# Gated delta block: one unscaled split of the residual for all projections, the norm's root multiplied in behind each projection

## The reference, cut to what matters

```python
def rmsnorm_2(x, g):
    y = xf * lax.rsqrt(jnp.mean(xf * xf, axis=-1, keepdims=True) + NORM_EPS)
    return y * g

hn = rmsnorm_2(h, pre_norm[0])
proj = hn @ w_in                      # q, k, v, z and the rows b, a
qkv = silu(causal_conv(qkv, conv_w))  # 4 taps, per channel
q, k = l2norm(q) * GDN_DK ** -0.5, l2norm(k)
beta, g = sigmoid(b), -exp(a_log) * softplus(a + dt_bias)
o = gated_delta_rule_chunked(q, k, v, beta, g)
return (rmsnorm(o) * silu(z)) @ w_out
```

## Time and profile before

| | |
|---|---|
| median of 3 runs | 1937.38 us (1934.7 to 1939.07) |
| the profiled execution | 1939.72 us, of which the span of the page is 1937.6 us |
| busy: PE, DVE, ACT, POOL | 95%, 52%, 43%, 35% of the span |
| the chain that ended last | PE 45%, DVE 6%, POOL 4%, issue 3%, ACT 3% |
| MLP ends, entry begins | 739.4 us |
| groups 0 to 3 begin on DVE | 770.25, 930.71, 1087.83, 1249.25 us |

### The profile page before, as it was taken

The page is one execution under the profiler, slowest core; times in us unless marked ns, Lnnn a source line. Parts: engine busy times, 40 slices in busy tenths (PEclk is TensorE's granted clock), DMA queues, the critical chain, the costliest instruction groups (busy, mean ns, idle before and its releaser), DMA issues.

```text
span 1937.6 us, 30475 instructions
## 1 busy us (share of the span) xinstructions
PE 1832.4 (95%) x11573; PEld 1530.8 (79%) x11709; DVE 1000.4 (52%) x1762; ACT 828.4 (43%) x1512; POOL 675.3 (35%) x429
## 2 busy tenths in 40 slices
PE   6999999999999998998999999999988999999996
PEld 4777788878787876896989998998876667777776
DVE  6522233641211125665765774775766556566666
ACT  4565652352323233633633642562545433333433
POOL 3222244353534342270280263255224222222312
PEclk9999999999999998999999999999999989999998
DMA  5111223232323230420230131132122111211211
GB/s 186 55 55 57 63 93 107 73 93 71 120 76 108 76 109 22 129 87 1 79 83 30 55 91 48 52 82 76 45 100 76 55 33 55 66 56 52 76 32 44
DMA packets 73669, 138.91 MB, mean 72 GB/s; under 512 B 30640, under 2 KB 42416, under 8 KB 73296
## 3 DMA queue, kind: packets, MB, share of 16 engines
q1 hardware_dynamic: 72976, 132.41, 22.6%
q10 hardware_dynamic: 576, 4.87, 0.6%
HBM read 127.62 MB, written 9.63 MB: 71 GB/s over the span
## 4 chain that ended last, share of the span: by engine, by line
PE 45%; DVE 6%; POOL 4%; issue 3%; ACT 3%; DMA 0%; SPq 0%; ACTq 0%; POOLq 0%; DVEq 0%
PE ps L349 9%; PE ps L351 8%; PE ps L350 8%; PE ps L3131 4%; PE ps L3087 2%; PE ps L3094 2%; POOL wsp L344 2%; PE ps L3121 1%; PE ps L2804 1%; POOL ov L855 1%; PE ps L2913 1%; PE ps L2946 1%; PE ps L2951 1%; DVE aux_f L1814 1%; PE ps L2938 1%
## 5 line engine op out<-in xcount | busy, mean ns | idle before, releaser
L344 POOL TENSOR_TENSOR wsp<-raw,wsp 128x1024 fp32r<-128x1024 f32 x228 | 549.5, 2416 | 1152.9 <-ACT wsp L339 1152.6
L349 PE MATMUL ps<-h_split,wsp 128*128 128x264 f32 (+2 forms) x1552 | 536.3, 346 | 15.8 <-DVE h_split L498 5.2
L350 PE MATMUL ps<-h_split,wsp 128*128 128x264 f32 (+2 forms) x1552 | 517.0, 333 | 0.0
L351 PE MATMUL ps<-h_split,wsp 128*128 128x264 f32 (+2 forms) x1552 | 516.3, 333 | 0.0
L349 PEld LDWEIGHTS ps<-h_split,wsp 128*128 128x128 f32 x1552 | 295.0, 190 | 57.3 <-issue 16.2
L350 PEld LDWEIGHTS ps<-h_split,wsp 128*128 128x128 f32 x1552 | 295.7, 191 | 29.2 <-issue 0.5
L351 PEld LDWEIGHTS ps<-h_split,wsp 128*128 128x128 f32 x1552 | 294.8, 190 | 29.3
L339 ACT ACTIVATE wsp<-raw 128x1024 fp32r<-128x1024 f32 x228 | 237.6, 1050 | 95.3 <-PE ps L351 94.5
L349 PE MATMUL ps<-y_split,wsp 128*128 128x512 f32 (+2 forms) x512 | 196.4, 383 | 11.5 <-DVE y_split L532 5.3
L350 PE MATMUL ps<-y_split,wsp 128*128 128x512 f32 (+2 forms) x512 | 192.4, 376 | 0.0
L351 PE MATMUL ps<-y_split,wsp 128*128 128x512 f32 (+2 forms) x512 | 192.0, 375 | 0.0
(11 more groups left out here) (397 smaller groups left out, 2929.0 us busy)
## 6 DMA issues: line engine op xcount, KB each, us to landing
raw<-in_w SPq DMA_DIRECT2D x228, 512.0 KB, 3.5
m_home<-ov SPq DMA_DIRECT2D x16, 256.0 KB, 4.2
x_home<-x_res ACTq DMA_DIRECT2D x1, 2112.0 KB, 6.9
x_res<-in_x SPq DMA_DIRECT2D x4, 512.0 KB, 5.5
out<-x_res SPq DMA_DIRECT2D x16, 128.0 KB, 1.7
x_res<-x_home ACTq DMA_DIRECT2D x1, 1584.0 KB, 7.2
mats<-in_mats SPq DMA_DIRECT2D x1, 640.0 KB, 7.4
x_res<-x_home ACTq DMA_DIRECT2D x1, 528.0 KB, 3.7
```

Of the source, the lines that this page charges most:

```text
L344: pool.tensor_tensor(wsp[:, s, 1, :], raw[:, s, :], wsp[:, s, 0, :].bitcast(F32), ALU.subtract).then_inc(lo_ready, 1)
L349: pe.matmul(o, wh, xh, start=start, stop=False)
L350: pe.matmul(o, wh, xl, start=False, stop=False)
L351: return pe.matmul(o, wl, xh, start=False, stop=stop)
```

## The change

The root is no longer part of `HS`. Behind nB's addition ACT squares each tile of `X` and writes the high part of X times gain at once, DVE the low part (`low_plain`). PE mixes the sums of squares with the first half of panels 0 and 1, then finishes panel 0, then `wba`, then panel 1. The root stands in `g_rs`, an SBUF tile of 528 columns in space left by constant matrices that are now last in their array. In each tile, DVE first writes PSUM times root into `QKV[:, t, :]` (`root`), and the four taps read from there; PE starts panel t + 2 behind this `root`. `copy_z` and the rows b and a take the root in the same way. Two panels' splits move from the group ahead of it, and the clearing of `accT` (POOL) behind the split of panel 5. One more DMA loads constants at the start.

```diff
+        g_rs = mats_all[:, (NMAT + 1) * P - T:(NMAT + 1) * P]
+        N3 = dict(sq=N2["sq"], rs=g_rs)
...
@@ sync
-            sp.dma_start(mats[:, 0:NEG_TRIL_16, :], A["mats"][:, 0:NEG_TRIL_16, :]).then_inc(sem("consts_in"), 16)
+            sp.dma_start(mats[:, 0:NEG_TRIU_16, :], A["mats"][:, 0:NEG_TRIU_16, :]).then_inc(sem("consts_in"), 16)
+            sp.dma_start(mats[:, NEG_TRI:NMAT, :], A["mats"][:, NEG_TRI:NMAT, :]).then_inc(sem("consts_in"), 16)
@@ gpsimd
+            split_low(pool, P_GDN + AHEAD)
             norm_add_odd(pool, "nB", N1, REAL)
-            pool.memset(F[:, 0:KT * T], 0.0).then_inc(sem("acc_zero"), 1)
...
-                for j in range(6):
+                for j in range(1 if first else 0, 6):
                     low(j)
+                    if first and j == 3:
+                        pool.memset(F[:, 0:KT * T], 0.0).then_inc(sem("acc_zero"), 1)
@@ scalar
+            split_high(act, P_GDN + AHEAD)
             norm_rsqrt(act, "nB", N1, False, to=PS[:, 7, :])
+            split_high(act, P_GDN + AHEAD + 1)
-            norm_squares(act, "n3", lambda k: X[:, k, :], N2, ready=lambda k: added("nB", k))
-            norm_rsqrt(act, "n3", N2, True)
-            norm_high(act, "n3", N2, hs(ALL))
+            for k in range(KT):
+                norm_square(act, "n3", lambda m: X[:, m, :], N3, k, lambda m: added("nB", m))
+                gained_high(act, "n3", k, HS[:, 0, k, :], X[:, k, :], "pre_norm_0")
+            norm_rsqrt(act, "n3", N3, True)
@@ vector
-            norm_apply(dve, "n3", lambda k: X[:, k, :], "pre_norm_0", N2, hs(ALL))
+            def low_plain(k):
+                gained_low(dve, "n3", k, HS[:, 1, k, :], X[:, k, :], "pre_norm_0", HS[:, 0, k, :])
+            norm_add(dve, "nB", lambda k: acc1[:, k, :], "g_post_mlp", N1, REAL, PS[:, 7, :], low_plain)
...
+                def root(t):
+                    tile_used(t)
+                    dve.tensor_tensor(two(QKV[:, t, :]), acc2(2 * (t % 2)), two(g_rs), ALU.mult)\
+                       .then_inc(sem("g_taps"), 1)
                 def taps(t):
-                    x, y = acc2(2 * (t % 2)), cv[t % 2]
+                    x, y = QKV[:, t, :], cv[t % 2]
-                    tile_used(t)
-                    dve.tensor_scalar(two(y[:, 0:T]), x, cwg[:, 4 * t + 3:4 * t + 4], None, ALU.mult)
+                    root(t)
+                    dve.wait_ge(*rooted(g, t))
+                    dve.tensor_scalar(y[:, 0:T], x, cwg[:, 4 * t + 3:4 * t + 4], None, ALU.mult)
...
                         dve.scalar_tensor_tensor(out=shifted, in0=x, scalar=cwg[:, 4 * t + k:4 * t + k + 1],
                                                  in1=shifted, op0=ALU.mult, op1=ALU.add)
...
-                    dve.tensor_copy(two(zrow[t]), acc2((0, 2, 6, 6)[t]))
+                    dve.tensor_tensor(two(zrow[t]), acc2((0, 2, 6, 6)[t]), two(g_rs), ALU.mult)
@@ tensor, first group
+                    for kt in range(KT):
+                        square_sum(kt)
+                        if kt % 2:
+                            early(0, kt // 2)
+                            early(1, kt // 2)
+                    for kt in range(4, KT):
+                        early(0, kt)
+                    ... wba, then early(1, 4), early(1, 5), gates_turned(), early(1, 6), early(1, 7)
+                    pe.wait_ge(*rooted(0, 0))
+                    project(2, 0, 0, 4)
                     decay_sums()
-                    project(1, 2, 6)
-                    pe.wait_ge(sem("g_conv"), 1)
-                    project(2, 0)
+                    project(2, 0, 4)
+                    pe.wait_ge(*rooted(0, 1))
+                    project(3, 2, 0, 4)
                     pe.wait_ge(sem("rows_moved"), 16 + 64)
@@ tensor, every group, each of panels 2 to 9
-                pe.wait_ge(sem("g_conv"), gst(g, 8, t))
+                pe.wait_ge(*rooted(g, t - 1))
```

More of the change, by code:

```diff
@@ L50 @@
 NCOL = sum(WIDTHS)
-(IDENT, TRI_U, NEG_TRI, NEG_ONES, ONES, MASK_SB, MASK_MLA, MEAN_D, MEAN_128, MEAN_256,
- NEG_TRIL_16, NEG_TRIU_16, META_LEVELS, LANE_LEVELS) = range(14)
+(IDENT, TRI_U, NEG_ONES, ONES, NEG_TRIL_16, MEAN_D, MEAN_128, MEAN_256, NEG_TRIU_16,
+ LANE_LEVELS) = range(10)
 LEVELS = 7
@@ L56 @@
 LANE_LEVEL = 4
-NMAT = LANE_LEVELS + LEVELS - LANE_LEVEL
+META_LEVELS = LANE_LEVELS + LEVELS - LANE_LEVEL
+NEG_TRI, MASK_SB, MASK_MLA = range(META_LEVELS + 1, META_LEVELS + 4)
+NMAT = MASK_MLA + 1
 SKEW = P * BLK + BLK
@@ L505, in norm_high, with norm_add @@
                 act.activation(at(0, kt), N["tmp"][kt % 2], ACT.Copy).then_inc(sem("norm_hi"), 1)
-        def norm_add(dve, tag, src, gain, N, c, rs):
+        def norm_add(dve, tag, src, gain, N, c, rs, after=None):
             dve.wait_ge(sem("norm_rs"), nth("norm_rs", tag, 1))
@@ L519, in norm_add @@
                        .then_inc(sem("norm_added"), 1)
+                if after is not None and kt >= 2:
+                    after(kt - 2)
+            if after is not None:
+                after(KT - 2)
+                after(KT - 1)
             dve.wait_ge(*added(tag, KT - 1))
@@ L1811, in taps @@
                         k = 3 - late
-                        shifted = two(y[:, late:late + T])
-                        dve.wait_ge(sem("g_taps"), gst(g, 24, 3 * t + late))
+                        shifted = y[:, late:late + T]
+                        dve.wait_ge(sem("g_taps"), gst(g, 32, 4 * t + late + 1))
                         dve.scalar_tensor_tensor(out=shifted, in0=x, scalar=cwg[:, 4 * t + k:4 * t + k + 1],
@@ L1883, in copy_z @@
                     tile_used(8 + t)
-                    dve.tensor_copy(two(zrow[t]), acc2((0, 2, 6, 6)[t])).then_inc(sem("z_copy"), 1)
+                    dve.tensor_tensor(two(zrow[t]), acc2((0, 2, 6, 6)[t]), two(g_rs), ALU.mult)\
+                       .then_inc(sem("z_copy"), 1)
                 group_taps()
@@ L1889, in gdn_group @@
                     taps(0)
+                    conv_clamp(0)
+                    rows_rooted()
                     gates_front()
-                    conv_clamp(0)
+                    gated(0)
+                    gates_end()
                     decay_low()
                     decay_rest()
-                    gated(0)
-                    dve.wait_ge(sem("ba_dve"), 9)
-                    dve.wait_ge(sem("ba_act"), 11)
+                    dve.wait_ge(sem("ba_dve"), 10)
+                    dve.wait_ge(sem("ba_act"), 10)
                     group_rows()
                 else:
+                    if g == 1:
+                        dve.wait_ge(sem("acc_zero"), 2)
                     group_rows()
@@ L2633, in gdn_group, with square_sum @@
                 if first:
+                    def square_sum(kt):
+                        pe.wait_ge(sem("norm_sq"), nth("norm_sq", "n3", kt + 1))
+                        for a in range(2):
+                            last = pe.matmul(PS[:, 4 + a, 0:HALF], mat(MEAN_D),
+                                             N3["sq"][kt % 2][:, a * HALF:(a + 1) * HALF],
+                                             start=kt == 0, stop=kt == KT - 1)
+                        last.then_inc(sem("norm_acc"), 1)
@@ L2635, in gdn_group, with early @@
+                    def early(j, kt):
+                        pe.wait_ge(*split_ready("n3", kt + 1))
+                        last = mm3t(pe, 2 * j, *part(j, kt), HS, kt, kt == 0, kt == KT - 1)
+                        if kt == KT - 1:
+                            last.then_inc(used, 1)
                     ready(0)
+                    ready(1)
                     for kt in range(KT):
-                        pe.wait_ge(*split_ready("n3", kt + 1))
+                        square_sum(kt)
+                        if kt % 2:
+                            early(0, kt // 2)
+                            early(1, kt // 2)
@@ L2638, in gdn_group @@
+                    for kt in range(4, KT):
+                        early(0, kt)
+                    for kt in range(KT):
                         w = [wba_all[:, half * 256 + 32 * kt:half * 256 + 32 * kt + P] for half in range(2)]
                         last = mm3t(pe, 6, *w, HS, kt, kt == 0, kt == KT - 1)
-                        if kt == KT - 1:
-                            last.then_inc(sem("ba_pe"), 1)
-                        last = mm3t(pe, 0, *part(0, kt), HS, kt, kt == 0, kt == KT - 1)
@@ L2643, in gdn_group @@
-                    last.then_inc(used, 1)
-                    project(1, 2, 0, 3)
+                    last.then_inc(sem("ba_pe"), 1)
+                    early(1, 4)
+                    early(1, 5)
                     gates_turned()
-                    project(1, 2, 3, 6)
+                    early(1, 6)
+                    early(1, 7)
+                    pe.wait_ge(*rooted(0, 0))
+                    project(2, 0, 0, 4)
                     decay_sums()
-                    project(1, 2, 6)
@@ L3259, in host_layout @@
     mats += level[LANE_LEVEL:]
+    order = (0, 1, 3, 4, 10, 7, 8, 9, 11, 13, 14, 15, 12, 2, 5, 6)
```

(1 more changed line is left out.)

96 lines of the change are left out of this document (48 added, 48 removed).

## The result

The changed kernel takes 1980.3 us (median of 4 runs, 1979.0 to 1983.0), the kernel before 1937.0 (1934.7 to 1939.1) on the same chip: ratio 1.0226, 95% interval 1.0208 to 1.0243. The forecast was 1977, slower. The profiled executions have spans of 1981.0 and 1937.6 us, 43.4 apart.

A forecast was written before the change was run, and what follows sets the result against it. The chain of DVE and ACT in turn and the lane chain, not PE at 95%, were taken to end each group. Terms sum to 39.7 us on 1939.7, giving 1979.4, less 2.3 for the median: 1977 us, range 1948 to 1993.

The forecast's parts named there:

- The port: SBUF-only taps wait for POOL's split: +2.3 us in tiles 1 and 2 of group 1, 2.2 in tile 3.
- Rival A: Taps are no dearer from SBUF than from PSUM and the port costs nothing: sum 0, 1937 us, chance 0.09.
- Rival B: Only taps behind the first L344 wait, tiles 1 and 2 of each group: some +16, 1953 us, chance 0.2.
- A tile undisturbed: Per tile without POOL: root product +0.75, first tap falling from 0.77 to about 0.44 (-0.33), +0.4 us in sum.
- To the last M: Up to each group's last M: +7.9 us in group 1, +6.4 in groups 2 and 3.
- Lane chain: From the last M to the first spread, POOL's lane steps and DVE's path: +4.1 us a group.
- Clock: PE, waiting before each level stage, restarts at a low clock: 1 us a group, between 0 and 2.
- Group 0 and the entry: Of 9 us won at panel 0, 3.5 reach the decay rows; last M at -1.6, with the lane chain +2.5.
- Rival C: The entry's whole 9 us reach the end, at group 0's decay rows: -6, 1931 us, chance 0.07.
- The signs: Changed profile: first tap 436 ns alone, lane steps' median over 0.4, group 1 12 us longer, PE waits before level stage.
- The sum: Whole kernel: 2.5 + (7.9 + 4.1) + 2 x (6.4 + 4.1) + 4 x 1 + 0.2 = 39.7 us.

The follow-up runs named there:

- runs 1, 2 and 3: 1: changed kernel, root product in place in PSUM, 1948.7 us; 2 and 3: kernel before plus a PSUM-to-SBUF copy per tile, not read 1947.6, read by taps 1988.3.
- the run of the second half: Kernel with the root product in place in PSUM (1948.7 us), but tiles 4 to 7 of each group tapped from SBUF: 1961.0 us, ratio 1.0124.
- run 5: Changed kernel, taps still from SBUF, but PE waits for a tile's last tap before it reuses the bank: 1980.6 us, ratio 1.0226.
- run 4: Changed kernel without the root product on the q, k and v tiles, taps reading PSUM, their weights scaled by 0.02: 1935.7 us, ratio 0.9988.
- Run 12: Kernel with the root product in place in PSUM (1948.7 us), group 0's second half of panel 3 moved into PE's decay wait: 1944.6 us, ratio 1.0047.
- run 11: Kernel before, with only the next tile's first tap issued between the clamp and the gated product: 1946.5 us, ratio 1.0052.

## Why the prediction was right

*The port.* Shown by runs 1, 2 and 3: the operand is worth 31.6 us in the new kernel and 40.7 in the old one, with equal instruction counts. Rival A, by which SBUF costs what PSUM does, is excluded by the same runs. (The Trainium skill, GPSIMD Engine Reference, section Key points, on SBUF interfaces shared with VectorE when an instruction has two SBUF inputs or runs in a two-port mode: the traces agree for the former, 768 to 2941 ns for the later taps. The first tap has one SBUF tensor and takes 494 to 2325; whether it runs in a two-port mode no row says. One case goes further than the sentence: beside POOL's clearing two SBUF inputs are not held, see the last section.) Rival B, in which only tiles 1 and 2 of a group pay, falls with the run of the second half: tiles 4 to 7 alone cost 12 us.

*A tile undisturbed.* Root product 0.70 as said. The first tap takes 0.50 alone, not 0.44. The neighbour that I read it from the earlier trace rows has a constant as its scalar and works in place, the tap has a column of SBUF as its scalar. It is not the place: an instruction of the latent layer that is in place too, but with such a column, takes what the tap takes:

```profile
1603.69 0.49 DVE L2289 TENSOR_SCALAR ov<-ov,tiny 128x528 f32<-128x528 f32 x1
```

So 0.75 - 0.27 = +0.5. (The Trainium skill, VectorE: DVE Perf Modes, section Rules for kernel authors, on copying PSUM to SBUF ahead of many operations: here the copy's 0.75 buys 0.27 on the first of four taps and nothing on the others, 768 against 770 ns.)

*To the last M.* Predicted +7.9 and twice +6.4, measured +7.9 and twice +6.3.

*Lane chain.* Predicted +4.1 a group; the lanes on POOL grew by exactly 4.1. The way from the last M to PE's level stage holds more than the lanes: DVE's own lateness ahead of them (+0.5), and the low split queued behind them (+0.3), for which PE waits. Measured +4.9 in every group, 19.5 against 16.4. I had followed DVE's path to the spreads; the path that ends last is POOL's split and PE's panel 9.

*Clock.* I took 1 us a group to reach the end, between 0 and 2. Windows over group 1, before and after (us; busy (x) of PE, PEld, DVE, ACT, POOL; PEclk, DMA, GB/s):

```profile
930.71:1087.83 157.12, 153.32 (x1432) 144.16 (x1465) 107.15 (x193) 76.33 (x136) 63.15 (x61) 1.00 0.23 66
```
```profile
937.65:1111.64 173.99, 159.82 (x1432) 150.07 (x1465) 122.73 (x202) 76.15 (x136) 66.94 (x61) 0.96 0.21 59
```

The same 1432 matmuls keep PE busy 6.5 us longer, at a clock of 0.96 instead of 1.00. What reaches the end is the third row of the table, 5.5 us in panel 9, up to 2.7 in one group, and at most the 1.2 of the fourth, which has both signs: some 6.7 against 4. This size is that of one execution; in run 5, with the same median time, only group 0 pays for panel 9 (7.54 us).

*Group 0 and the entry.* PE starts the first projection at 751.1 (forecast: by 750). The wait for the decay rows is 2.65 instead of 3 to 4, then 2.98 more for the decays themselves. The last M came at -0.4 instead of -1.6; behind it come +4.9 to the end of the split and +1.2 in panel 9. The port works at the entry too, which the prediction left out: the last low part of `HS` meets a split that the change has put there and takes 2.03 us instead of 0.76 (761.62, beside 760.25 to 763.08). Rival C, in which all 9 us arrive, is excluded by run 4: even without the product they don't. Run 12 shows one way in which they get lost: of the 1.9 us by which the l2 scaling starts earlier, POOL's split takes 1.0.

*The signs.* Four of those named came out otherwise than said. The lane steps have medians of 386 and 443 ns (L869, L865), not both over 400; the first tap alone takes 494 and not 436; group 1 is longer by 16.9 us and not 12; and PE's waits of some us stand before panel 9 and not before the level stage.

*The sum.* 39.7 forecast, 0.2 of them at the kernel's start; the layer has +46.2: 1.0 more to the last M, 3.1 more from there to the end of the split, 2.7 more for the clock. Outside the layer 1.3 and -4.1 make it 43.4 between the profiles; the part behind the layer differs as much between runs with the same code there, so I hold these two for differences between executions. That the forecast of 1977 is only 3 us off is therefore partly luck; that it lies on the right side by this mechanism is not.

## What to carry to other kernels

In these traces a DVE instruction with a PSUM operand is immune to GpSimd's SBUF work, and one with all operands in SBUF that starts beside a GpSimd instruction with SBUF inputs waits for the whole of it, so before moving a chain of operations from PSUM to SBUF, look at what GpSimd has at that very phase. If two engines are released by the same event, the collision comes back in each group and not at random, and a shift by 0.7 us can bring it to another instruction. A multiplication that is saved once and added per tile pays only if the tile's chain isn't the bound: here it was, although its engine was busy 52% of the time.

## What the runs showed that I had not expected

- An element-wise product written back in place into PSUM takes 708 ns, into SBUF 701 ns (128x528, fp32): keeping the result in PSUM costs 7 ns an instruction here.
- A split of 2.4 us makes the tap beside it up to 2.17 us longer (2941 against 770 ns), while the 63 splits of the layer keep a median of 2365 ns, with 2832 at most: the two don't share by halves, DVE waits for the whole of POOL's instruction. Short POOL steps beside taps take 0.7 to 0.8, the length of a tap.
- Issuing one tap 0.7 us earlier in DVE's idle time made the kernel before 0.5% slower (run 11).
- One POOL instruction holds up no pair of SBUF inputs: the clearing of `accT`, which only writes. In group 0 an l2 scaling with two SBUF tensors keeps its 0.71 us beside it, while the first tap, with one, takes 0.74 instead of 0.50 and ends 0.29 behind it:

```profile
800.76 3.63 POOL L873 MEMSET work<- 128x4224 f32 x1
```
```profile
801.96 0.71 DVE L1859 SCALAR_TENSOR_TENSOR work<-work,ov 128x528 f32<-128x528 f32 x1 [5.00 <-ACT ov L1224]
...
803.94 0.74 DVE L1836 TENSOR_SCALAR aux_f<-work,cwg 128x528 f32<-128x528 f32 x1
```
